# Prompt attention: exponentials written over their input, reciprocal sums spread out by VectorE and turned by four transposes, and the turning and scaling two units later

## The reference, cut to what matters

```python
def sparse_attend(q, ks, vs, valid):
    qg = q.reshape(b, nq, N_KV_HEADS, N_HEADS // N_KV_HEADS, HEAD_DIM)      # 16 heads of 64, 4 key heads
    s = jnp.einsum('bqhgd,bqnhd->bqhgn', qg, ks).astype(jnp.float32) * HEAD_DIM ** -0.5
    s = jnp.where(valid[:, :, None, None, :], s, -jnp.inf)
    p = jax.nn.softmax(s, axis=-1).astype(vs.dtype)
    o = jnp.einsum('bqhgn,bqnhd->bqhgd', p, vs)
    return o.reshape(b, nq, ATTN_WIDTH)
```

## Time and profile before

| | |
|---|---|
| median of 3 runs | 3562.2 us (3560.37 to 3564.01) |
| the profiled execution's own time | 3561.58 us |
| its span in the profile | 3559.9 us |
| PE busy | 3435.1 us (96%) |
| DVE busy | 2035.5 us (57%) |
| ACT busy | 768.8 us (22%) |
| POOL busy | 1542.5 us (43%) |
| mean granted TensorE clock | 0.974 of full |

### The profile page before, as it was taken

The page is one execution under the profiler, slowest core; times in us unless marked ns, Lnnn a source line. Parts: engine busy times, 40 slices in busy tenths (PEclk is TensorE's granted clock), DMA queues, the critical chain, the costliest instruction groups (busy, mean ns, idle before and its releaser), DMA issues.

```text
span 3559.9 us, 57261 instructions
## 1 busy us (share of the span) xinstructions
PE 3435.1 (96%) x22646; PEld 3251.3 (91%) x22646; DVE 2035.5 (57%) x3072; ACT 768.8 (22%) x1585; POOL 1542.5 (43%) x675
## 2 busy tenths in 40 slices
PE   8999999999899999999889889999999999999998
PEld 7999999998898899999677647889999999999998
DVE  5333334346667999998676545986392533334324
ACT  2000000003232211233566414762100200000000
POOL 3533443342333344444367315984443333443451
PEclk9999999999999999999799977999999999999999
DMA  2111111112212222222223227943251111111111
GB/s 91 54 47 35 47 55 39 41 53 73 57 42 78 79 91 94 84 91 92 72 78 102 83 69 192 248 113 119 85 186 42 49 47 35 51 55 35 41 59 54
DMA packets 392987, 272.45 MB, mean 77 GB/s; under 512 B 54970, under 2 KB 368650, under 8 KB 392856
## 3 DMA queue, kind: packets, MB, share of 16 engines
q1 hardware_dynamic: 373032, 225.76, 22.3%
q10 hardware_dynamic: 19824, 44.95, 3.4%
HBM read 211.05 MB, written 59.81 MB: 76 GB/s over the span
## 4 chain that ended last, share of the span: by engine, by line
PE 90%; DVE 3%; POOL 2%; issue 2%; ACT 1%; DMA 1%; DVEq 0%; SPq 0%; ACTq 0%; POOLq 0%
PE setB L365 10%; PE setB L366 10%; PE setA L365 10%; PE setB L367 10%; PE setA L366 10%; PE setA L367 10%; PE bankC L365 2%; PE bankC L367 2%; PE bankC L366 2%; PE bankD L367 2%; PE bankD L365 2%; PE bankD L366 2%; PE setB L517 1%; PE bankC L1535 1%; PE bankD L2155 1%
## 5 line engine op out<-in xcount | busy, mean ns | idle before, releaser
L345 POOL TENSOR_TENSOR whi<-wraw,ones 128x1024 fp32r<-128x1024 f32 x190 | 465.0, 2447 | 1604.3 <-PE setA L367 1024.3
L365 PE MATMUL setA<-hhi,whi 128*128 128x352 f32 (+1 forms) x2304 | 751.0, 326 | 17.4 <-POOL wlo L348 8.4
L365 PE MATMUL setB<-hhi,whi 128*128 128x352 f32 (+1 forms) x2304 | 747.7, 325 | 1.9 <-POOL wlo L348 1.9
L366 PE MATMUL setA<-hlo,whi 128*128 128x352 f32 (+1 forms) x2304 | 744.3, 323 | 0.0
L367 PE MATMUL setA<-hhi,wlo 128*128 128x352 f32 (+1 forms) x2304 | 743.6, 323 | 0.0
L366 PE MATMUL setB<-hlo,whi 128*128 128x352 f32 (+1 forms) x2304 | 741.8, 322 | 0.0
L367 PE MATMUL setB<-hhi,wlo 128*128 128x352 f32 (+1 forms) x2304 | 740.8, 322 | 0.0
L348 POOL TENSOR_TENSOR wlo<-wraw,whi 128x1024 fp32r<-128x1024 f32 x190 | 480.4, 2528 | 14.9
L365 PEld LDWEIGHTS setA<-hhi,whi 128*128 128x128 f32 x2304 | 435.1, 189 | 31.2 <-issue 15.6
L365 PEld LDWEIGHTS setB<-hhi,whi 128*128 128x128 f32 x2304 | 433.0, 188 | 11.1 <-ACT spill L1007 6.5
L366 PEld LDWEIGHTS setA<-hlo,whi 128*128 128x128 f32 x2304 | 435.1, 189 | 1.7
(11 more groups left out here) (423 smaller groups left out, 5706.5 us busy)
## 6 DMA issues: line engine op xcount, KB each, us to landing
wraw<-in_w_in SPq DMA_DIRECT2D x64, 512.0 KB, 3.8
wraw<-in_w_ffn_gate SPq DMA_DIRECT2D x44, 512.0 KB, 3.8
wraw<-in_w_ffn_up SPq DMA_DIRECT2D x44, 512.0 KB, 3.8
wraw<-in_w_ffn_down SPq DMA_DIRECT2D x44, 512.0 KB, 3.4
abc<-acsD SPq DMA_DIRECT2D x8, 2048.0 KB, 11.2
xcD<-cv ACTq DMA_DIRECT2D x24, 520.0 KB, 2.7
zD<-spill ACTq DMA_DIRECT2D x16, 524.0 KB, 2.7
sraw<-sD SPq DMA_DIRECT2D x2, 4192.0 KB, 13.0
```

Source lines behind the costliest of these rows:

```text
L345: pool.tensor_tensor(dst_cols(slot, hi), dst_cols(slot), ones[:, :].unsqueeze(1).to_broadcast([P, KD, P]), ALU.mult).then_inc(w_hi, 1)
L365: pe.matmul(out, w1, r1, start=start, stop=False)
L366: pe.matmul(out, w1, r2, start=False, stop=False)
```

## The change

Four things change together.

- `pr` is gone. The exponential is written over its input, `smx`, and the transposes read `smx`. So ACT no longer waits, before an exponential, for the transposes of the unit two (or four) earlier (`pt_done`), and DVE, before a mask, waits for these transposes instead of for that unit's exponential.
- DVE spreads the eight reciprocals into `rlx`, 64 copies of each (a copy of 128x512, behind a wait for the reciprocal).
- PE turns them by four 128x128 transposes instead of eight matmuls of 64 columns.
- The turn, `copy_out` and `result` stand at u = 11, 19, ..., 131 instead of u = 9, 17, ..., 129. `recip` stays at u = 8, 16, ...

The core of the diff:

```diff
         smx = a.take("smx", [P, 2, L])
-        pr = a.take("pr", [P, 2, L])
         ptT = a.take("ptT", [P, 4, NT, P])
+        rlx = a.take("rlx", [P, 8, HD])
...
-                    if bank == 0 and u > 8:
-                        pe.wait_ge(ot_evac, (u - 1) // 8)
+                    if bank == 0 and u > 10:
+                        pe.wait_ge(ot_evac, (u - 3) // 8)
                     for b in range(nb):
                         mm = pe.transpose(CD[bank][0:kn, b * P:(b + 1) * P],
-                                          buffer(pr, u, (b0 + b) * P, (b0 + b) * P + kn), ident[:, :])
+                                          buffer(smx, u, (b0 + b) * P, (b0 + b) * P + kn), ident[:, :])
...
                 for k in range(n):
-                    for h in range(2):
-                        mm = pe.matmul(bankC[h * HD:(h + 1) * HD, k * P:(k + 1) * P],
-                                       rl[:, 2 * k + h:2 * k + h + 1].to_broadcast([P, HD]), ident[:, :],
-                                       start=True, stop=True)
+                    mm = pe.transpose(bankC[:, k * P:(k + 1) * P],
+                                      rlx[:, 2 * k:2 * k + 2, :].rearrange("p h d -> p (h d)"), ident[:, :])
...
-                if u % 8 == 1 and u > 8:
+                if u % 8 == 3 and u > 8:
                     turn_recip(u // 8 - 1, u, 4)
...
-                if u >= ahead(u):
-                    wait_both(act, pt_done, u - ahead(u) + 1)
...
-                act.activation(buffer(pr, u, 0, w), buffer(smx, u, 0, w), ACT.Exp, bias=nmax[:, u % 4:u % 4 + 1],
+                act.activation(buffer(smx, u, 0, w), buffer(smx, u, 0, w), ACT.Exp, bias=nmax[:, u % 4:u % 4 + 1],
...
-                if u % 8 == 1 and u > 8:
+                if u % 8 == 3 and u > 8:
                     copy_out(u // 8 - 1)
...
-                    v.wait_ge(exp_done, u - ahead(u) + 1)
+                    wait_both(v, pt_done, u - ahead(u) + 1)
...
-                v.reciprocal(rl[:, 0:n], lsum[:, i // 2 % 2, i % 2 * 8:i % 2 * 8 + n]).then_inc(rl_ready, 1)
+                ch.run(v.reciprocal(rl[:, 0:n], lsum[:, i // 2 % 2, i % 2 * 8:i % 2 * 8 + n]))
+                v.tensor_copy(rlx[:, 0:n, :], rl[:, 0:n].unsqueeze(2).to_broadcast([P, n, HD])).then_inc(rl_ready, 1)
...
-                if u % 8 == 1 and u > 8:
+                if u % 8 == 3 and u > 8:
                     result(u // 8 - 1)
```

More of the change, by code:

```diff
@@ L207, in build @@
         smx = a.take("smx", [P, 2, L])
-        pr = a.take("pr", [P, 2, L])
         ptT = a.take("ptT", [P, 4, NT, P])
+        rlx = a.take("rlx", [P, 8, HD])
+        a.take("spare", [P, 8320 // 4 - 8 * HD])
         kidxg_off = a.cur
```

## The result

| kernel | median us | lowest to highest | runs |
|---|---|---|---|
| before | 3562.3 | 3558.98 to 3565.22 | 8 |
| changed | 3568.3 | 3564.27 to 3576.11 | 8 |

The account below looks back on a forecast made before the run. It took ACT's `copy_out` to time the long turns, PE's reciprocal waits being only 5.9 us. Terms -2.4 - 2.5 + 0 + 1.5 + 4.2 + 1.3 = +2.1 us on 3562.2 gave 3564, range 3552 to 3573.

Parts of the forecast that it names:

- block term: DVE's spreading copy, held by POOL's operations in seven places: +4.2 us; 0 if not blocked, 12.9 if nothing is hidden.
- Rival B: The copy is blocked by POOL seven times and nothing hides it: 9.4 us for blocks, +13 in all, 3575; 18%.
- Rival A: The savings arrive: shorter turns and reciprocal waits all count, 13 us, copy never blocked, 3549; 22%.
- Part 1: PE's turn by four transposes: 0.46 us shorter each, nothing in eight long turns, gains in short tiles; -2.4 us.
- Part 2: Turn two units behind the reciprocals: PE's big wait of 4.7 us at (7,1) goes; -2.5 us, between 0 and -4.7.
- Part 3: Without `pr`, ACT's waits for `pt_done` go and DVE's replace them, already over when reached: 0.
- Part 4: DVE's spreading copy: 0.48 us plus 0.1 of wait; +1.5 for its length and +4.2 for blocks by POOL.
- about 1.05 are free each time: Of each blocked copy, DVE hides 0.5 us and PE has 0.55 us of room, leaving 6.65 us over seven.
- so they vanish: The 2.45 us of block ahead of (6,15) cost nothing, since DVE waits 2.62 us for POOL there anyway.
- +1.5 of its own: The copy's plain length on DVE: 0.58 us hidden in long tiles, 0.2 each in seven short ones.
- Part 5: What the moved turn, `copy_out` and `result` pass, such as query copies and state sums: +1.3 us, bounds -2 and +5.
- Rival C: POOL sets the pace from tile 6's second query copy to (6,15), so changes there vanish: 3562 within 3; 12%.

Follow-up runs that it names:

- kernel 1: The changed kernel with the reciprocals spread into `rlx` by a `tensor_reduce` instead of a copy: 3555.8 us, ratio 0.9981.
- kernel 4: The changed kernel with the old turn of eight matmuls reading `rl` and no spreading copy: 3560.8 us, ratio 0.9996.
- kernel 8: Kernel 1 with ACT's `copy_out` issued ahead of the next unit's exponential instead of behind it: 3550.2 us, ratio 0.9960.
- kernel 9: Kernel 4 with `copy_out` issued ahead of the next unit's exponential: 3555.5 us, ratio 0.9974.
- Kernel 5: The changed kernel with turn, `copy_out` and `result` back at their old place: 3576.1 us, ratio 1.0036.
- kernel 3: The kernel before with only the exponentials written over their input: 3564.7 us, ratio 1.0001.
- kernel 7: Kernel 1 with a second reduce of 0.69 us, into a buffer nothing reads, ahead of the real one: 3568.3 us, ratio 1.0015.
- kernel 2: The kernel before with only turn, `copy_out` and `result` two units later: 3561.5 us, ratio 0.9994.
- kernel 12: The kernel before with DVE's `key_low` of unit (2,9) taken one unit earlier, at (2,8): 3562.0 us, ratio 0.9998.

## Why the prediction was right, and where only its sum was

**The class and the time** held, 3568 against 3564 in a range of 3552 to 3573. That the sum held was luck: two terms were too small, with opposite signs. Kernel 1, which has everything but the block, prices them: 8 us under before, where the prediction has 2.1 - 4.2 = -2.1 without its block term; and the blocks cost 12.5, not 4.2. Rival B's 9.4 was nearer on the price of the blocks. Rival A's 13 was a little nearer on the savings, but by a mechanism that kernels 1, 4, 8 and 9 exclude: the long turns were held by `copy_out`.

**Part 1, the turn.** Right in mechanism for the long turns: they gain nothing (6.46 for 6.48 us), since ACT's `copy_out` times `result`. Kernels 1, 4, 8 and 9 show it: the same 0.46 us count only once `copy_out` is early. In the short tiles no gain of the turn can be seen in the timelines: up to unit 56 kernel 1 won 7.1 us and kernel 4, with the old turn, 7.5. What the shorter turn alone is worth (I had 2.4) stays open: between kernels 4 and 1 the medians say 5.0 us in its favour, and the two timelines 0.6 against it within the attention stretch.

**Part 2, the reciprocals.** Right: no wait of the turn for them. At (7,1), units 112 to 120, the changed kernel won 2.6 us; I had -2.5 for the reciprocals and +1.95 for the copy blocked there. Kernel 1, whose spread isn't blocked, won 2.4 at the same place, so the saving was sized well and the block of 3.0 us cost nothing. Kernel 5 is the same statement turned round: with the copy and without the move 23.7 us of waits.

**Part 3, no `pr`.** Right: kernel 3 differs from before by a ratio of 1.0001 (0.9992 to 1.0010).

**Part 4, the copy.** The free copy took 0.43 (I had 0.48), seven were blocked, as listed: over 0.43 they had 1.8, 3.2, 1.1, 0.9, 0.1, 3.4 and 3.0 us, where I had 1.3, 3.0, 1.1, 0.9, 0.1, 3.5 and 3.0. The step that failed is "about 1.05 are free each time", with "so they vanish" for tile 6. Against kernel 1, the block of 3.2 us at 1825.22 cost 3.9, with no discount, where I had 1.95. The one in tile 6 cost 2.2, where I had nothing: DVE's wait for POOL did shrink, from 2.62 to 0.62 us, but the copy (1949.21, 3.86 us) stood ahead of masks that PE needed first. At 1795.09 the copy pushed a `key_low` behind the start of POOL's next operation, so that 1.8 us of block cost 4.7, where I had 0.25. What I had priced was a late engine; what the block does is to change which later operations are blocked. My "+1.5 of its own" for the copy's plain length can't be read off: kernel 7 shows that a plain 0.69 us costs nothing in the last six turns, as I said, and many times its length in tiles 1 and 2, where the timelines show the same thing: a DVE operation that now starts inside a POOL one.

**Part 5, the order.** By the traces the sign was wrong. I had +1.3; the move as a whole is a gain of 2 to 4 us by the medians of kernels 2 and 4 (where parts 2 and 5 together had -1.2) and 7 to 8 in their profiled executions. The costs that I listed for the query copy did come: the periods with the first turns of tiles 4, 5 and 6 are 6.92, 7.24 and 7.78 us in the changed kernel, 6.13, 6.43 and 6.90 before. But 4.2 us were won at a place that my list of "what moves past what" passed over: `result`, at (2,11) instead of (2,9), no longer stands ahead of the first of the two `key_low`. I listed what the three moved steps pass on ACT and PE, and not what DVE's other work passes on POOL. That this is the cause is read from the timelines and not shown; kernel 12 missed the place by 0.41 us. That the profiled executions of kernels 2 and 4 are the quickest of their eleven, and their others up to 11 us slower, fits a step that is caught in some executions and missed in others, but no trace of a slower one is at hand, so it stays open.

**Rival C** put POOL's pace into tile 6. Kernel 12 finds it at the end of tile 2, in one mask; kernel 1, 8 us faster with the same work on POOL, shows that it doesn't bound the stretch.

**The signs to look for** that the prediction gave all came: the turn of 0.63, `result` behind `copy_out` in 12 of 16 (I had nearly all), a wait for `qT` (0.81 at the turn shown; I had 0.5), short and long copies (two of the long ones under the 1.5 us I had), no 4.7 us, a period of 6.5.

## What to carry to other kernels

Before adding an operation to DVE while POOL works in SBUF, look at its form first and its length second: a spread that took 0.69 us as a reduction was worth 12.5 us over one that took 0.43 as a copy. A blocked operation's price isn't what is left of POOL's operation: list what is queued behind it on DVE, and see whether any of that slips past the start of POOL's next one. And when a step is shortened without effect, as the long turns were here, see which engine's instruction ends last beside it; moving `copy_out` ahead of one exponential took 5.6 us off kernel 1 and made the fastest version, 3550 us.

## What the hardware showed that I had not expected

The price of DVE's time was uneven within one loop: 0.69 us more at each half tile cost 10.6 us of the attention stretch up to unit 84, and 0.0 over the six half tiles behind it (kernel 7).

A DVE `tensor_tensor` with both inputs in SBUF took 0.70 us undisturbed and 4.72 us when begun 0.41 us into a POOL `tensor_tensor` (kernel 12). In the other order it was POOL that stretched: 4.12 us for 3.65 when DVE's had begun 0.57 us ahead of it (kernel 2), having itself been held until POOL's operation before ended. The Trainium skill names this pair as well (SBUF — State Buffer, "Who interferes with whom"): two SBUF inputs on DVE contend with a GpSimd instruction that reads SBUF, and the first to issue has the ports. Both orders here agree. I had cited it for the new copy and had not applied it to the `key_low` that the copy pushes.

The four transposes of 128x128 f32 took 0.63 us, and 1.12 at the lower clock level, which the changed kernel still had at its turn at 1830.60, right behind the block at 1825.22 (granted clock 0.66 from 1829 to 1834), while kernel 1 ran all its turns from tile 1 on in 0.63 to 0.66.
